# A decoder layer on one core: index low parts between scores, a later small sum, and block sums on GpSimd

## The reference

```python
proj = x @ w_in[layer]
q, k, v, qi, ki, wi, gate_b, gate_c, h = _split_cols(proj, IN_SPLIT_SIZES)
# q, k, qi, ki are rotated (rope); 8 heads of 64 for attention, 8 index heads of 64 with one key
# per block of 128 queries:
dots = jnp.einsum('bqhd,bsd->bqhs', qi_b, ki32) * (IDX_DIM ** -0.5)
score = jnp.einsum('bqh,bqhs->bqs', w_b, jax.nn.relu(dots))        # w_b = wi * 8 ** -0.5
score = jnp.where(admissible[None], score, -jnp.inf)               # causal
_, idx = lax.top_k(score, 256)                                     # 256 keys a query
# softmax attention of q over the selected k, v -> attn_out
conv_out = gate_b * causal_dwconv3(gate_c * h)
mixed = concat(rms_norm(attn_out), rms_norm(conv_out)) * gains
x = layer_norm(ALPHA * x + mixed @ w_out)
gate, up = jnp.split(x @ w_gate_up, 2, axis=-1)                    # D_FF = 2816
x = layer_norm(ALPHA * x + (jax.nn.silu(gate) * up) @ w_down)
```

## Time and profile before

| | |
|---|---|
| median of 3 runs | 1262.85 us |
| profiled execution | 1260.8 us, of it the span from first to last instruction 1259.0 us |
| TensorE busy | 1224.8 us (97%), 6037 matmuls |
| VectorE busy | 958.3 us (76%) |
| GpSimd busy | 661.8 us (53%) |
| ScalarE busy | 521.0 us (41%) |
| chain that ended last | TensorE 89%, VectorE 6%, ScalarE 2% |
| granted TensorE clock, mean | 0.997 of full speed |

### The profile page before, as it was taken

One profiled execution on the slowest core, in us unless ns is written; L12 is line 12 of the kernel. 1 busy time (PEld: TensorE's weight loads), 2 busy tenths in 40 slices (PEclk: granted clock), 3 DMA queues, 4 the chain that ended last, 5 costly groups with the idle time before them and its releaser, 6 DMA issues.

```text
span 1259.0 us, 17040 instructions
## 1 busy us (share of the span) xinstructions
PE 1224.8 (97%) x6037; PEld 1030.0 (82%) x6037; DVE 958.3 (76%) x1549; ACT 521.0 (41%) x911; POOL 661.8 (53%) x544
## 2 busy tenths in 40 slices
PE   8989999999998999999999999999999999999997
PEld 7967788888887899788778888888888888888885
DVE  3687999999978889437867776776776766565897
ACT  4375322221339789503533323333323333553351
POOL 2240666698779541108678666666666630020744
PEclk9999999999999999999999999999999999999999
DMA  5231222211002112424135545544445448966664
GB/s 202 72 89 33 51 51 60 67 33 46 24 17 52 35 28 74 160 74 152 51 127 167 175 139 172 175 142 160 161 134 191 159 152 292 358 190 196 198 189 166
DMA packets 121404, 157.66 MB, mean 125 GB/s; under 512 B 7252, under 2 KB 81256, under 8 KB 119912
## 3 DMA queue, kind: packets, MB, share of 16 engines
q1 hardware_dynamic: 121320, 156.57, 38.8%
HBM read 109.09 MB, written 40.11 MB: 119 GB/s over the span
## 4 chain that ended last, share of the span: by engine, by line
PE 89%; DVE 6%; ACT 2%; issue 2%; DMA 1%; POOL 0%; SPq 0%; DVEq 0%; ACTq 0%; POOLq 0%
PE banks L694 26%; PE banks L696 26%; PE banks L695 26%; PE banks L908 2%; PE banks L959 2%; DVE scores L1886 1%; PE banks L859 1%; PE banks L927 1%; PE banks L928 1%; PE banks L876 1%; PE banks L877 1%; PE banks L710 1%; DVE pt L1983 1%; PE banks L1036 0%; DMA xs<-in_x 0%
## 5 line engine op out<-in xcount | busy, mean ns | idle before, releaser
L1902 DVE TENSOR_SCALAR_CACHE_REDUCE mask<-scores,small 128x384 bf16<-128x384 f32 (+1 forms) x186 | 163.7, 943 | 1.1
L2235 DVE TENSOR_TENSOR step_lo<-step_raw,step_hi 128x1024 fp32r<-128x1024 f32 x77 | 110.4, 1454 | 57.0 <-ACT step_hi L1455 56.2
L1689 POOL TENSOR_TENSOR ring_lo<-sum,ring_hi 128x512 fp32r<-128x512 f32 x88 | 122.0, 1389 | 59.8 <-ACT ring_hi L1390 59.7
L694 PE MATMUL banks<-act_hi,ring_hi 128*128 128x512 f32 x352 | 137.0, 389 | 0.0
L696 PE MATMUL banks<-act_hi,ring_lo 128*128 128x512 f32 x352 | 136.9, 389 | 0.0
L695 PE MATMUL banks<-act_lo,ring_hi 128*128 128x512 f32 x352 | 136.9, 389 | 0.0
L1689 POOL TENSOR_TENSOR ring_lo<-gu_raw,ring_hi 128x512 fp32r<-128x512 f32 x66 | 94.4, 1431 | 73.2 <-ACT ring_hi L1390 73.2
L1455 ACT ACTIVATE step_hi<-step_raw 128x1024 fp32r<-128x1024 f32 x77 | 81.7, 1061 | 111.0 <-DMA step_raw<-in_w_down 56.1
L1390 ACT ACTIVATE ring_hi<-sum 128x512 fp32r<-128x512 f32 x88 | 55.1, 630 | 161.7 <-POOL sum L1700 61.8
L694 PE MATMUL banks<-step_hi 128*128 128x512 f32 x308 | 119.9, 389 | 0.0
L696 PE MATMUL banks<-step_hi,step_lo 128*128 128x512 f32 x308 | 119.8, 389 | 0.0
(11 more groups left out here) (268 smaller groups left out, 3159.3 us busy)
## 6 DMA issues: line engine op xcount, KB each, us to landing
gu_raw<-in_w_gate_up SPq DMA_DIRECT2D x44, 512.0 KB, 5.2
step_raw<-h_store SPq DMA_DIRECT2D x77, 256.0 KB, 3.0
wd_raw<-in_w_down SPq DMA_DIRECT2D x11, 1024.0 KB, 5.0
h_store<-hid SPq DMA_DIRECT2D x11, 1024.0 KB, 3.9
step_raw<-wd_store SPq DMA_DIRECT2D x44, 256.0 KB, 3.6
wd_store<-wd_raw SPq DMA_DIRECT2D x11, 768.0 KB, 3.4
h_store<-h_sum SPq DMA_DIRECT2D x11, 768.0 KB, 5.4
step_raw<-in_w_down SPq DMA_DIRECT2D x33, 256.0 KB, 3.1
```

The source lines that it names most:

```text
L694: pe.matmul(dst, a[0], b[0], start=first, stop=False)
L1689: pool.tensor_tensor(ring_lo[:, slot], src, ring_hi[:, slot].bitcast(F32), ALU.subtract).then_inc(ring_low, 1)
L1902: c = dve.tensor_scalar(mask[:, part(b)], scores[:, part(b)], threshold(j), 0.0, ALU.is_ge, ALU.add, accum_out=count[:, j:j + 1])
L2235: dve.tensor_tensor(step_lo[n][:], step_raw[n][:], step_hi[n][:].bitcast(F32), ALU.subtract).then_inc(step_low, 1)
```

## The change

The low parts of an index block are no longer made at the end of the block two before, but inside the block just before it: behind head 0's score the first query part, behind head 1's the second and the key's. The causal term of a block is added behind head 3's score of the next block. The second part of the last small sum loses its copy and its sum to `join_last_small`, one step later, behind that step's low parts. `sum_hidden` is GpSimd's now for pairs 0 to 9: in the preparation of unit 2i + 3, behind its fourth low part. The last pair's stays with VectorE.

```diff
 # GpSimd
+            def sum_hidden(i):
+                a11, a21, a12, a22 = (quarter(hid, f, half) for f in range(2) for half in range(2))
+                pool.wait_ge(h_done, 4 * i + 4)
+                if i:
+                    pool.wait_ge(h_stored, 32 * i)
+                pool.tensor_tensor(h_sum[:, 0, :], a21, a22, ALU.add).then_inc(h_summed, 1)
+                pool.wait_ge(h_summed, 4 * i + 1)
+                pool.tensor_tensor(h_sum[:, 1, :], h_sum[:, 0, :], a11, ALU.subtract).then_inc(h_summed, 1)
+                pool.tensor_tensor(a21, a11, a21, ALU.subtract).then_inc(h_summed, 1)
+                pool.wait_ge(h_summed, 4 * i + 2)
+                pool.tensor_tensor(h_sum[:, 2, :], a12, h_sum[:, 1, :], ALU.subtract).then_inc(h_summed, 1)
             for u in range(1, UNITS):
...
                 last_sums(u)
                 ring_low_of(u, 3)
+                if u % 2 and u >= 3:
+                    sum_hidden((u - 3) // 2)
                 if u >= 2:
                     ring_low_of(u, 4)
 # VectorE, indexer: idx_low(b) is now query_low(b, 0); query_low(b, 1); key_low(b)
+            def add_causal(b):
+                n = (b + 1) * P
+                s = scores[:, OFF[b]:OFF[b] + n]
+                dve.wait_ge(score_added, (b - SEL[0] + 1) * HEADS)
...
+                link(dve.tensor_tensor(s[:, b * P:n], s[:, b * P:n], causal[:], ALU.add))
...
-                dve.wait_ge(score_added, i + 1)
-                if b == SEL[0]:
-                    dve.wait_ge(const_made, 1)
-                link(dve.tensor_tensor(s[:, b * P:n], s[:, b * P:n], causal[:], ALU.add))
-                if b + 2 < NB:
-                    idx_low(b + 2)
-
+                    if b > SEL[0] and h < 2 and b + 1 < NB:
+                        query_low(b + 1, h)
+                        if h == 1:
+                            key_low(b + 1)
+                    if b > SEL[0] and h == 3:
+                        add_causal(b - 1)
+            add_causal(NB - 1)
 # VectorE, attention
                 dve.tensor_tensor(high, high, scale, ALU.mult).then_inc(halves_scaled, 1)
-                dve.wait_ge(halves_scaled, b + part + 1)
                 if part == 0:
+                    dve.wait_ge(halves_scaled, b + 1)
                     dve.tensor_tensor(target, high, target, ALU.add).then_inc(half_summed, 1)
-                else:
-                    dve.wait_ge(half_summed, 1)
-                    dve.tensor_copy(o_row[:, 0:half, :], half_row[:])
-                    dve.tensor_tensor(target, high, target, ALU.add).then_inc(heads_summed, 1)
+
+            def join_last_small():
...
+                dve.wait_ge(half_summed, 1)
+                dve.tensor_copy(o_row[:, 0:half, :], half_row[:])
+                dve.wait_ge(halves_scaled, b + 2)
+                dve.tensor_tensor(target, OUT_SMALL[b % 2][:, half:HEADS, 0, :], target, ALU.add
+                                  ).then_inc(heads_summed, 1)
...
                 if i == LARGE0 + 3:
                     sum_last_small(1)
+                if i == LARGE0 + 4:
+                    join_last_small()
 # VectorE, combine of the gate and up stage
-                if part == 0 and i:
-                    sum_hidden(i - 1, "s1")
-                    sum_hidden(i - 1, "s2")
-                elif part:
+                if part:
                     sum_down(i, "t2")
...
-                if part == 0 and i:
-                    sum_hidden(i - 1, "s3")
-                    sum_hidden(i - 1, "s4")
-                elif part:
+                if part:
                     sum_down(i, "t4")
```

More of the change, by code:

```diff
@@ L1849, in rotate_first_heads, with query_low, key_low @@
                 dve.wait_ge(idx_rotated, b - SEL[0] + 1)
-            def idx_low(b):
+            def query_low(b, odd):
                 dve.wait_ge(idx_hi, b + 1)
-                q_bank, k_bank = IDX_BANKS.get(b, (4, 5))
+                q_bank, own = IDX_BANKS.get(b, (4, 5))[0], half_of(odd)
                 if q_bank is not None:
-                    for odd in range(2):
-                        own = half_of(odd)
-                        dve.tensor_tensor(qi_lo[own, b % 2, odd::2, :],
-                                          ps[own, q_bank, :].rearrange("p (c s) -> p c s", c=CT),
-                                          qi_hi[own, b % 2, odd::2, :].bitcast(F32), ALU.subtract)
+                    dve.tensor_tensor(qi_lo[own, b % 2, odd::2, :],
+                                      ps[own, q_bank, :].rearrange("p (c s) -> p c s", c=CT),
+                                      qi_hi[own, b % 2, odd::2, :].bitcast(F32), ALU.subtract)
+            def key_low(b):
+                k_bank = IDX_BANKS.get(b, (4, 5))[1]
                 lower = ki_hl[HD:P, b * P:(b + 1) * P]
@@ L1869, in _, with idx_low @@
             rotate_first_heads(3)
+            def idx_low(b):
+                query_low(b, 0)
+                query_low(b, 1)
+                key_low(b)
+            def add_causal(b):
+                n = (b + 1) * P
+                s = scores[:, OFF[b]:OFF[b] + n]
+                dve.wait_ge(score_added, (b - SEL[0] + 1) * HEADS)
+                if b == SEL[0]:
+                    dve.wait_ge(const_made, 1)
+                link(dve.tensor_tensor(s[:, b * P:n], s[:, b * P:n], causal[:], ALU.add))
             for b in range(3):
@@ L2019, in sum_last_small @@
                 dve.tensor_tensor(high, high, scale, ALU.mult).then_inc(halves_scaled, 1)
-                dve.wait_ge(halves_scaled, b + part + 1)
                 if part == 0:
+                    dve.wait_ge(halves_scaled, b + 1)
                     dve.tensor_tensor(target, high, target, ALU.add).then_inc(half_summed, 1)
-                else:
-                    dve.wait_ge(half_summed, 1)
-                    dve.tensor_copy(o_row[:, 0:half, :], half_row[:])
-                    dve.tensor_tensor(target, high, target, ALU.add).then_inc(heads_summed, 1)
+            def join_last_small():
+                b, half = SMALL - 1, HEADS // 2
+                target = o_row[:, half:HEADS, :]
+                dve.wait_ge(half_summed, 1)
[3 more added lines that the diff above has]
+                                  ).then_inc(heads_summed, 1)
             def sum_heads(b):
```

## The result

The kernel after takes 1265.51 us (median of 22 runs, 1262.76 to 1266.84), the kernel before, in 22 runs too, 1262.14 us (1259.66 to 1264.26). The ratio is 1.0025, with a 95% interval of 1.0019 to 1.0030: +3.2 us by the ratio, +3.4 by the medians. The profiled execution of after took 1266.37 us, with a span of 1264.6, 5.6 us more than the profiled one of before.

A forecast was written before the change was run, and what follows sets the result against it. TensorE was taken as the bound, busy 1224.8 of 1259.0 us. Terms 1.05 + 2.24 - 0.7 + 0 = +2.6 us on a median of 1262.85 gave 1265.4 us; 8-in-10 range 1262.8 to 1267.6.

The forecast's parts named there:

- Block entries, +1.05: Indexer, entering blocks 3, 4 and 5: VectorE idles 0.9 us, 0.55 is hidden between scores, +0.35 each, +1.05 us.
- The rival in which nothing is hidden (+2.7): Indexer block entries: moved instructions overlap nothing, costing 2.7 us there; total +4.5, 1267.4 us; chance 8%.
- TensorE's wait for idx_lo, +2.24: Indexer block 6: the first extra convolution matmul waits for the last key low part, now later, +2.24 us.
- Clock, no term: Whole kernel: granted clock is 1.00 in both windows and TensorE's work is unchanged, so no clock cost.
- the 3 to 3.5: Sign at the end of the indexer stage: it ends 3 to 3.5 us later than before.
- its other signs: Block 6 wait about 2 us, VectorE idle about 0.9, attention waits 1.5 to 0.5, TensorE busy throughout gate and up.
- Join, -0.7: Attention, last small sum: low parts start 0.94 us sooner, of which 0.7 remains, -0.7 us.
- The 0.24 that was taken off for the next unit: Attention, one unit on: only 0.7 of the 0.94 us gain was expected to remain.
- GpSimd, 0: Gate and up stage: four sums take about 5.5 us on GpSimd, within 8.9 us of slack, so 0 us.
- the 7.2 that the prediction drew from the shared read interface: Gate and up stage: four sums at 1.8 us each take 7.2 us on GpSimd, the term still 0.
- Transfers of the low parts, 0: Indexer: block 6's copies land 1.3 us before its dots, cost 0, up to +1 per block if landing takes 3.5.
- a chance of 0.52: Whole kernel: chance given to the change being slower by over 0.2%.

The follow-up runs named there:

- e1: Kernel before with only the index low parts and causal addition moved between the next block's scores: 1266.42 us, ratio 1.0033.
- e4: Kernel before with index low parts and causal addition moved, but block 7's low parts left at their old place: 1262.96 us, ratio 1.0006.
- e9: Kernel before with index low parts and causal addition moved, and TensorE's extra convolution passes starting at head 4 instead of 2: 1262.56 us, ratio 1.0002.
- e2: Kernel before with only the last small sum's copy and sum moved one step later in attention: 1261.77 us, ratio 0.9994.
- e3: Kernel before with only the four sums of gated value blocks moved from VectorE to GpSimd: 1262.40 us, ratio 1.0001.
- e12: Same program as e7, executed and profiled once more: stage end 69.68 us behind the first score against 68.04.
- e8: Kernel before with only block 7's low parts moved, behind block 6's third score (head 2): 1267.81 us, ratio 1.0049.
- e7: Kernel before with only block 7's low parts moved, behind block 6's second score (head 1): 1266.61 us, ratio 1.0045.

## Why the prediction was right

The forecast was 1265.4 us, +2.6 us; 1265.51 and +3.4 (2.4 to 3.8) were measured. Its steps one by one:

- **Block entries, +1.05.** Measured +1.02 (after) and +1.03 (e1). Block by block it is not as even as priced (0.35 each). The last score of block 3 ends 0.17 us later than in before, that of block 4 0.57 and that of block 5 1.02. The idle time ahead of the first score, priced at 0.9, was 0.59, 0.98 and 0.92 us, and 0.42, 0.58 and 0.47 of it came back between the scores, priced at 0.55. That the sum is right within 0.03 us is in part luck: block 3's entry was overpriced and the next two underpriced. The rival in which nothing is hidden (+2.7) fell. The half of the rule of the Trainium skill (VectorE: DVE Perf Modes, The DRAIN you can't avoid) by which an operation that isn't held starts earlier holds between scores too: 0.07 us in the rows above.
- **TensorE's wait for idx_lo, +2.24.** Measured +2.28, with the releaser that was named; e4 and e9 remove it in two ways, and it goes.
- **Clock, no term.** This step failed. "TensorE's work doesn't change, so the clock has no term in the sum": the work is the same, but the new wait is a reason of its own, and cost +1.52 us in the profile of after and 1.58 in e1. Because of it the stage ended 4.82 us later and not the 3 to 3.5 that the prediction names among its signs; its other signs came true. Before's trace has half a warning, if one looks where TensorE waits for long and not only at the two windows of the earlier trace rows. Behind its wait of 2.2 us, which ends at 621.89, the clock stayed at 1.00; at the one of 1.7 us, which ends at 631.43, it fell (windows of before, columns as above):

```profile
619.00:630.00 11.00, 7.88 (x54) 5.44 (x52) 10.36 (x18) 8.90 (x18) 5.14 (x5) 1.00 0.12 48
630.00:634.00 4.00, 2.57 (x6) 2.09 (x7) 2.57 (x5) 2.69 (x5) 4.00 (x4) 0.65 0.38 101
```

- **Join, -0.7.** Measured -0.97 (after), -0.97 (e2). The sign and place were right, and the whole of the 0.94 us by which the low parts start sooner came through. The 0.24 that was taken off for the next unit was not lost: TensorE's next transposes come 2.07 us on in both kernels (435.73 to 437.80, and 441.19 to 443.26).
- **GpSimd, 0.** Measured 0.00 (e3), with VectorE's waits for the store at 65.3 us and none of them passed on. The four sums took 6.0 us in the rows above, between the 5.5 that were priced and the 7.2 that the prediction drew from the shared read interface at 1.8 us each, a figure that no row has.
- **Transfers of the low parts, 0.** In after TensorE doesn't wait for one; in e1 it did once for 0.4 us, without effect on the distance. The slack of 1.3 us was worked out for block 6; that wait is ahead of block 4, where there was less.

By these steps the profile has 1.02 + 2.28 + 1.52 - 0.97 = +3.85 where the clock falls, and +2.3 where it doesn't. The measured 3.4 lies between: the forecast of +2.6 came out at 1265.4 because the median that it was added to, of three runs, lies 0.7 us above that of all 22. That made up for nearly all of the 0.8 us by which the step was too small, so the agreement of the times within 0.1 us is luck. The ratio, 0.25%, lies above the bound of 0.2% that the chances use, with an interval from 0.19 to 0.30%; one outcome says little about a chance of 0.52.

No version here beats before by a margin that the times show. The later join alone (e2) is the best by the trace, 0.97 us ahead; by its times it is -0.8 us with zero inside the interval.

## What to carry to other kernels

Where an operand is moved later, look for the one instruction that waits for the last of a count, and ask whether it can stand later instead: here two heads later saved what three moved instructions had cost. A new wait of some 2 us on a busy TensorE is to be priced at its length and, with a chance, at some 1.5 us of lowered clock behind it. And an engine's idle hole is only worth filling if what goes into it is ready in it: the low parts wait for ScalarE's high parts, which are the hole.

## What the runs showed of the hardware

- TensorE's granted clock fell from the 2.4 to the 1.2 GHz level 0.2 to 0.9 us behind the end of a wait of 2.1 to 2.4 us and stayed there for 3.4 us in after, e1 and e12; in after, 0.73 us of waiting had ended 1.3 us before that wait. Where the wait was 3.63 us (e8) the clock fell during it and stayed low for 6.8 us. In before it fell at a wait of 1.7 us (631.43), and not behind one of 2.2 us (621.89), so the length of the wait alone doesn't decide it. At the low level a 128x512 matmul took 0.63 us, spaced 0.43, against 0.39 and 0.23.
- One and the same program had the fall in one execution (e12) and not in another (e7), behind the same wait of 2.37 us: a difference of 1.64 us at the stage's end. Near 622 to 632 us the profiles split in the same way, by 1 us. The start varies by 2.4 us (65.9 to 68.3). Both could be a good part of the 4.6 us between the shortest and the longest run of before, though no rows of the timed runs show it, and both are the reason to read a difference below 1 us from distances in the trace.
- On GpSimd the four sums take 1339 to 1695 ns in the mean (lines 1759 to 1764 in after), 54.3 us for nine pairs. On VectorE three of them took 1663 to 1772 ns and the first 678, 52.4 us for the same. What stands beside GpSimd's operations there now pays: the first of VectorE's sums of the down weights went from 731 ns to 1502, while the second of the sums of the gate and up weights went from 1469 to 1032. The Trainium skill (SBUF — State Buffer, Who interferes with whom) has the shared read interface as the reason, and these means agree with it. Most of the cost of meeting GpSimd moved from one line to another: the six groups of weight sums that stay on VectorE took 84.6 us before and 80.5 after. The groups of VectorE in after, 635 to 1003 us (busy us, mean ns, idle before):

```profile
L2234 DVE TENSOR_TENSOR sum<-sum,gu_raw 128x512 f32<-128x512 f32 x20 | 20.6, 1032 | 0.7
...
L2257 DVE TENSOR_TENSOR wd_sum<-wd_raw 128x512 f32<-128x512 f32 x10 | 15.0, 1502 | 0.0
```
